# A gated weight's products cut into quarters of 256 tokens and laid between the turns of the tiles

## What is computed

```python
h = _rmsnorm(x, norm_g[layer]) * (1.0 + scale) + shift
proj = h @ w_in[layer]
(glu_a, glu_b, z_conv, q, k, v, z_att, g_conv, g_att) = jnp.split(proj, split_idx, axis=-1)
u = glu_a * jax.nn.sigmoid(glu_b)
u = lax.conv_general_dilated(u, conv_w[layer][:, None, :], window_strides=(1,), ...)
```

## Time and profile before

| what | value |
|---|---|
| median of 3 runs | 2903.88 us (2903.24 to 2905.91) |
| the profiled execution's own time | 2902.55 us |
| its span, first to last instruction | 2900.7 us |
| TensorE busy | 2809.1 us, 97% of the span |
| VectorE, ScalarE, GpSimd busy | 1783.9, 1245.5, 459.8 us |
| mean granted clock of TensorE | 0.992 of full |

### The profile page before, as it was taken

One profiled execution on the slowest core, in us unless ns is written; L12 is line 12 of the kernel. 1 busy time (PEld: TensorE's weight loads), 2 busy tenths in 40 slices (PEclk: granted clock), 3 DMA queues, 4 the chain that ended last, 5 costly groups with the idle time before them and its releaser, 6 DMA issues.

```text
span 2900.7 us, 36531 instructions
## 1 busy us (share of the span) xinstructions
PE 2809.1 (97%) x14556; PEld 2322.1 (80%) x14556; DVE 1783.9 (61%) x2498; ACT 1245.5 (43%) x2011; POOL 459.8 (16%) x423
## 2 busy tenths in 40 slices
PE   8999999999999999999988999999999999999998
PEld 7978888867884788888877888888888878588898
DVE  4645888322436788888874777777777664110564
ACT  4234787232221677777765124454443342011101
POOL 1500221000001211111114000000001063132241
PEclk9999999999999999999998999999999999999999
DMA  4130000411216999999973121030201221010141
GB/s 146 52 127 15 30 1 6 182 60 66 73 44 241 361 393 395 397 397 396 396 259 132 58 95 52 19 113 27 98 28 34 97 66 65 20 54 30 44 145 59
DMA packets 141461, 382.30 MB, mean 132 GB/s; under 512 B 11743, under 2 KB 45025, under 8 KB 141164
## 3 DMA queue, kind: packets, MB, share of 16 engines
q1 hardware_dynamic: 125036, 324.17, 29.6%
q0 software_dynamic: 13520, 46.28, 5.0%
q10 hardware_dynamic: 2736, 9.50, 0.9%
HBM read 340.47 MB, written 39.46 MB: 131 GB/s over the span
## 4 chain that ended last, share of the span: by engine, by line
PE 69%; DVE 7%; ACT 2%; issue 1%; DMA 1%; POOL 1%; ACTq 0%; POOLq 0%; DVEq 0%
PE ps L2750 7%; PE ps L2751 7%; PE ps L2752 7%; PE ps L2735 6%; PE ps L2737 6%; PE ps L2736 6%; PE ps L2365 4%; PE ps L2379 4%; PE ps L2815 2%; PE ps L2860 2%; PE ps L2817 2%; PE ps L2816 2%; PE ps L2829 1%; PE ps L2831 1%; PE ps L2830 1%
## 5 line engine op out<-in xcount | busy, mean ns | idle before, releaser
L2143 DVE SCALAR_TENSOR_TENSOR b_f<-b_f,small_f 128x1023 f32<-128x1023 f32 (+14 forms) x240 | 304.2, 1268 | 65.8 <-ACT small_f L1225 37.2
L2750 PE MATMUL ps<-x_f32r,w_f32r 128*128 128x512 f32 x480 | 187.8, 391 | 0.9 <-issue 0.8
L2752 PE MATMUL ps<-x_f32r,w_f32r 128*128 128x512 f32 x480 | 186.8, 389 | 0.0
L2736 PE MATMUL ps<-w_f32r,a_f32r 128*128 128x512 f32 x456 | 177.4, 389 | 0.0
L2365 PE MATMUL ps<-small_f 128*128 128x128 f32 (+1 forms) x984 | 135.5, 284 | 28.9 <-DMA b_f<-acc 11.6
L2751 PE MATMUL ps<-ht_f32r,w_f32r 128*128 128x512 f32 x416 | 161.9, 389 | 0.0
L2816 PE MATMUL ps<-w_f32r,a_f32r 128*128 128x512 f32 x384 | 150.0, 391 | 0.0
L2365 PEld LDWEIGHTS ps<-small_f 128*128 128x128 f32 (+1 forms) x984 | 117.5, 144 | 38.5 <-DMA b_f<-acc 12.0
L2750 PE MATMUL ps<-ht_f32r,w_f32r 128*128 128x512 f32 x320 | 124.9, 390 | 2.4 <-DVE x_f32r L2117 2.4
L2752 PE MATMUL ps<-ht_f32r,w_f32r 128*128 128x512 f32 x320 | 124.5, 389 | 0.0
L2736 PE MATMUL ps<-x_f32r,a_f32r 128*128 128x512 f32 x312 | 121.6, 390 | 0.0
(11 more groups left out here) (508 smaller groups left out, 7905.1 us busy)
## 6 DMA issues: line engine op xcount, KB each, us to landing
w_f<-in_w_exp_up SPq DMA_DIRECT2D x40, 1024.0 KB, 9.5
w_f<-in_w_exp_down SPq DMA_DIRECT2D x38, 1024.0 KB, 8.4
w_f<-in_w_exp_gate SPq DMA_DIRECT2D x36, 1024.0 KB, 8.0
x_f<-in_w_exp_gate SPq DMA_DIRECT2D x28, 1024.0 KB, 8.0
x_f<-in_w_exp_down SPq DMA_DIRECT2D x26, 1024.0 KB, 9.5
x_f<-in_w_exp_up SPq DMA_DIRECT2D x24, 1024.0 KB, 9.4
w_f<-in_w_in SPq DMA_DIRECT2D x22, 1024.0 KB, 5.1
w_f<-in_w_in SPq DMA_DIRECT2D x10, 2048.0 KB, 7.8
```

The source lines that it names most:

```text
L2143: ins = v.scalar_tensor_tensor(C_conv[k][:, d:S], U_conv[k][:, 0:S - d], cols[:, k, R_TAP + j:R_TAP + j + 1], C_conv[k][:, d:S], ALU.mult, ...
L2736: mm(o, x1, w2[:, k, c], start=False, stop=False)
L2750: mm(o, l1, r1, start=(k == 0), stop=False)
L2752: ins = mm(o, l2, r1, start=False, stop=(k == n - 1))
```

## The change

Weight 0's products are cut into quarters of 256 tokens (q = 0 to 3). Each quarter of each of its four (name, c) pairs is 24 matmuls of 128x256 into one half of a bank; the quarters 0 and 1 share the bank of h = 0, the quarters 2 and 3 that of h = 1. TensorE's new order: behind the turns of tile 2 come the two b quarters 0, behind those of tile 3 the two a quarters 0, behind tile 4 b 1, behind tile 5 a 1, behind tile 6 b 2, behind tile 7 a 2, and then all four quarters 3. A quarter q waits for `n4_split` 4(q + 1), that is for the tiles 2q and 2q + 1. Spare turns stay only ahead of the tiles 0 to 2. The turns use the banks 4 to 7 alone, so that the quarters have the banks 0 to 3 (and 4 and 5 for a of h = 1). ScalarE takes the two sigmoids of h = 0 behind its copies of tile 5. VectorE's program stays as it is.

```diff
--- before.py
+++ after.py
@@ -444,13 +444,22 @@
 
         GLU = [(nm, 0, c, h) for h in range(2) for nm in "ba" for c in range(2)]
         GLU += [(nm, i, c, h) for i in range(1, 4) for nm in "ba" for c, h in QUAD]
+        QUARTER = [(nm, c) for nm in "ba" for c in range(2)]
+
+        def quarter_steps(t):
+
+
+            q, part = divmod(t - 2, 2)
+            return [] if t < 2 else [(nm, c, q) for nm, c in QUARTER[2 * part:2 * part + 2]]
+
+        QUARTER_BANK = {("b", 0): (0, 0), ("b", 1): (1, 1), ("a", 0): (2, 4), ("a", 1): (3, 5)}
         for t in range(T):
-            if t >= T // 2:
-                nm, i, c, h = GLU[t - T // 2]
-                bk.add((f"glu_{nm}", i, c, h), bank=t - T // 2)
             for j in range(2):
-                bk.add(("n4", t, j), bank=2 * t + j if t < T // 2 else 4 + 2 * (t % 2) + j)
-        for nm, i, c, h in GLU[T // 2:]:
+                bk.add(("n4", t, j), bank=4 + 2 * (t % 2) + j)
+            for nm, c, q in quarter_steps(t):
+                if q % 2 == 0:
+                    bk.add((f"glu_{nm}", 0, c, q // 2), bank=QUARTER_BANK[nm, c][q // 2])
+        for nm, i, c, h in GLU[8:]:
             bk.add((f"glu_{nm}", i, c, h))
         def keys_of(g, tile):
 
@@ -1537,6 +1546,14 @@
                     act.wait_ge(sem("n4a_ssq"), t)
                 square(XB[:, t, :], D, st[:, 84 + t:85 + t], n4_junk[min(t, 1)]).then_inc(sem("n4a_ssq"), 1)
 
+            def gated(i, pos, c, h):
+                b = bk.wait(act, ("glu_b", i, c, h))
+                n = 4 * i + pos
+                if n >= 6:
+                    bk.read(act, ("glu_a", (n - 6) // 4, *QUAD[(n - 6) % 4]))
+                ins = nc.scalar.activation(sig[n % 6], PS[:, b, :], ACT.Sigmoid)
+                bk.done(ins, ("glu_b", i, c, h))
+
             first_square(0)
             first_square(1)
             for t in range(T + 1):
@@ -1556,6 +1573,9 @@
                             kk = 4 * j + k
                             ins = nc.scalar.activation(n4_tmp[(2 * u + j) % 4][:, c], PS[:, b, c], ACT.Identity, bias=affine[:, KC + kk:KC + kk + 1], scale=affine[:, kk:kk + 1])
                         bk.done(ins, ("n4", u, j))
+                    if u == 5:
+                        for c in range(2):
+                            gated(0, c, c, 0)
             act.wait_ge(sem("n4_split"), 2 * T)
 
             def chunk_out(k, part):
@@ -1580,12 +1600,8 @@
                     if i == 3 and pos == 2:
                         bk.read(act, ("glu_a", 2, 1, 0)), bk.read(act, ("glu_a", 2, 1, 1))
                         chunk_out(5, U[5])
-                    b = bk.wait(act, ("glu_b", i, c, h))
-                    n = 4 * i + pos
-                    if n >= 6:
-                        bk.read(act, ("glu_a", (n - 6) // 4, *QUAD[(n - 6) % 4]))
-                    ins = nc.scalar.activation(sig[n % 6], PS[:, b, :], ACT.Sigmoid)
-                    bk.done(ins, ("glu_b", i, c, h))
+                    if i > 0 or h > 0:
+                        gated(i, pos, c, h)
                 if i < 3:
                     first_hi(2 * i + 2)
                 else:
@@ -2765,23 +2781,38 @@
 
             def glu(nm, i, c, h):
                 split_wait(f"g{nm}{i}")
-                if i == 0:
-                    if c == 0 and nm == "b":
-                        spare_turns((f"glu_{nm}", i, c, h), 30)
-                    pe.wait_ge(sem("n4_split"), T + T * h)
                 feature_major((f"glu_{nm}", i, c, h), f"g{nm}{i}", c, h, ht_1)
 
+            def glu_quarter(nm, c, q):
+                h, part = divmod(q, 2)
+                name = (f"glu_{nm}", 0, c, h)
+                split_wait(f"g{nm}0")
+                pe.wait_ge(sem("n4_split"), 4 * (q + 1))
+                if part == 0:
+                    bk.begin(pe, name)
+                o = PS[:, bk.at[name][0], 256 * part:256 * part + 256]
+                w1, w2 = split_views(f"g{nm}0")
+                x1, x2 = (x[:, :, 256 * q:256 * q + 256] for x in ht_1)
+                for k in range(KC):
+                    mm(o, w1[:, k, tile(c)], x1[:, k, :], start=(k == 0), stop=False)
+                    mm(o, w1[:, k, tile(c)], x2[:, k, :], start=False, stop=False)
+                    ins = mm(o, w2[:, k, tile(c)], x1[:, k, :], start=False, stop=(k == KC - 1))
+                if part == 1:
+                    bk.end(ins, name)
+
             for t in range(T):
-                if t >= T // 2:
-                    glu(*GLU[t - T // 2])
                 if t == 0:
                     pe.wait_ge(sem("x_tile0"), XB_IN)
-                if t < T // 2:
-                    spare_turns(("n4", t, 0), 38 if t == 0 else 12)
+                if t < 3:
+                    spare_turns(("n4", t, 0), (38, 12, 12)[t])
                 pe.wait_ge(sem("n4b_hn"), t + 1)
                 for j in range(2):
                     turns(("n4", t, j), HN[t % 2][:, NB * j:NB * j + NB])
-            for g in GLU[T // 2:]:
+                for step in quarter_steps(t):
+                    glu_quarter(*step)
+            for nm, c in QUARTER:
+                glu_quarter(nm, c, 3)
+            for g in GLU[8:]:
                 glu(*g)
 
             def gate(u):
```

## The result

The changed kernel takes 2890.14 us (median of 5 runs, 2888.15 to 2892.86), against 2905.91 (2903.24 to 2908.25) for the kernel before beside it. The ratio of the runs is 0.9948, 95% interval 0.9937 to 0.9960: 15.1 us less, 11.6 to 18.3. Forecast were 2889.4 us and 14.5 less.

The account below looks back on a forecast made before the run. TensorE bounds the kernel, busy for 97% of the span. Quarters 46.1, turns 4.6 and clock 0.8 sum to 51.5 us against 66.0, so weight 1 starts 14.5 earlier: 2889.4 us, range 2885.5 to 2894.

Parts of the forecast that it names:

- The start: Norm stage: quarter 0 starts at 1543.45, just behind VectorE's last split of tile 1, which ends at 1543.42.
- The price of 256 columns: Quarters on TensorE: 384 matmuls 0.120 us apart cost 46.1, which is 2.5 more than the 43.6 of the halves.
- Rival 4: Quarters run at another rate: gain gone above 0.158 us between starts; at 1.2 GHz 46 more, 2935.4 us; chance 0.04.
- Turns: TensorE's turns of tiles 3 to 7 cost 0.92 us each, 4.6 in all.
- The clock: Quarter 0: its first 1.6 us run at half rate, losing 0.8 us; bounds 0 and 1.7 more.
- The sign "granted clock 1.00 from about 1545 on": Listed among the signs of a right forecast: TensorE at full clock from about 1545 us, early in the quarters.
- S: Stretch from tile 1's last split to weight 1's first product: 66.0 us before, predicted 51.5.
- Covers: Norm stage: splits, scaled tiles, banks and the sigmoids' table load are ready in time, so TensorE never waits for them.
- rival 1: ScalarE's chain stops TensorE now and then: 4.5 us lost, 2893.9 us; chance 0.15 together with VectorE's lateness not being absorbed.
- the thinnest slack: Weight 1's split takes 5.0 us after the last b quarter, TensorE needs it after 5.76: slack 0.75.
- What is behind the stage moves along: Behind weight 0, VectorE's sum and the v weight's fetch move along; nothing is tied to a time of its own.
- Rival 3: Something behind the stage, a fetch or the v weight, has its own time: no gain, 2903.9 us; chance 0.03.

Follow-up runs that it names:

- e2: Changed kernel with ScalarE's two sigmoids of h = 0 behind the copies of tile 6 instead of tile 5; 6.1 us less than the kernel before.
- e5: Changed kernel with the last four quarters in the order a, a, b, b instead of b, b, a, a; 6.1 us less than the kernel before.
- e6: Changed kernel with four convolution taps moved from weight 2's stretch to weight 1's, making VectorE late; median 2890.11 us.
- e1: Changed kernel with h = 1 products whole again behind tile 7's turns, after 30 spare turns; 8.4 us less than the kernel before.
- e7: Changed kernel without the stage's 38, 12 and 12 spare turns; 2890.07 us.
- e3: Changed kernel with 28 instead of 12 spare turns ahead of tile 2's turns and 6 behind them; median 2887.71 us.

## Why the prediction was right

- **The start.** Quarter 0 starts 0.10 behind the last split of tile 1 (1545.88 against 1545.78), where the prediction had 0.03.
- **The price of 256 columns.** Starts are 0.120 apart (1549.32, 1549.44), 384 of them 46.1. The term stands; that the 2.5 us over the halves is the price of loading the weights twice as often, as the prediction says, is not shown by any run. The formula of the Trainium skill that was weighed against it (TensorE: Matmul & The Clock Gate, "Back-to-back issue gap", 0.109) doesn't describe this stream; the row decides. That section of the Trainium skill gives the formula for a single matmul by itself, which the prediction leaves out. The estimate by the formula, 16.5, was 2.4 above the 14.1 of the profile. Rival 4 would have needed 0.158. Its price for the whole stage at the half clock was too high: it doubled 0.120 to 0.240, but the slow starts are 0.213 apart, and the slow turns that it leans on are 0.204 to 0.115, not twice. With 0.213 the loss would be 36 and not 46.
- **Turns.** A lap is 6.63; without its 5.76 it is 0.87, five times 4.4, against 4.6.
- **The clock.** Predicted 0.8, measured 1.4: 16 matmuls at 0.213 in the changed kernel. The size was off by 0.6: in the profile of before the half rate began with the turns of tile 2 (0.204 each), here those eight still took 1.09 in all and the half rate fell wholly on the first quarter. It is within the bounds given, as are the 0.5 to 2.4 of the other executions. The sign "granted clock 1.00 from about 1545 on" did not come: it was 0.50 from 1546 to 1548, and the slow starts end at 1549.2. That is the clock of 0.50 within the quarters that was to point to rival 4, but it lasted for 3.3 us of the 52.
- **Sum.** 46.1 + 4.4 + 1.4, with the 0.1 at the start, are 52.0, which is S; predicted 51.5.
- **Covers.** All held, and rival 1 with its waits did not come. The splits were ready in time, the table load is hidden (e2 shows by how little: one place later and 4.55 are idle), the thinnest slack is 0.84 against 0.75 (e5 shows what stands behind it). VectorE's last multiplication of weight 0 starts at 1601.17, 3.4 behind its product, and 0.44 of idle time is left at 1625.34; e6 shows that even without it nothing is lost.
- **What is behind the stage moves along.** VectorE's sum of the two parts and ScalarE's v weight, the rows of the changed kernel (VectorE, then ScalarE):

```profile
1723.23 0.69 DVE L2180 TENSOR_TENSOR b_f<-ps,a_f 128x512 f32<-128x512 f32 x1 [4.75 <-PE ps L2768]
...
1729.83 4.43 DVE L2207 TENSOR_TENSOR ht_f<-ht_f32r,x_f32r 128x4096 f32<-128x4096 f32 x1
```

```profile
1738.42 1.06 ACT L1627 ACTIVATE b_f32r<-w_f 128x1024 fp32r<-128x1024 f32 x1 [17.76 <-DMA w_f<-in_w_in]
```

The sum comes 11.7 earlier on the clock of the trace, that is 14.1 less the late start of 2.4; the v weight 11.4 earlier. Rival 3 is out. The same wait for the fetch is there (17.76 for 17.50): it hangs on a product and came along.

That the median landed 0.7 us from the forecast is partly luck: S was 0.5 longer than predicted, the clock's part of it can come out 1 us to either side in another execution, and the kernel before ran at 2905.91 in the larger set of runs, 2.0 above the median that the forecast started from.

## What to carry to other kernels

When the busiest engine waits in a stage that comes tile by tile, count its work and its waits separately: the most a new order can give is the waits, and it gives them if at every step the next piece's inputs are ready within a lap of work. Cutting products to half their width is cheap where the distance of starts nearly halves (0.227 to 0.120, 2.5 us for 384 matmuls), since it lets work start two tiles earlier. Then look for what the old wait hid: here a sigmoid with its table load and the split of the next weight, whose places had about 2 us and 0.8 us to spare. And when two profiles differ by a microsecond or two, first take out what each lost to the clock.

## What the hardware showed that I had not expected

- Nearly the same wait of TensorE (2.04 us before, 2.06 after, in the window stage) was followed by the full clock in one profile (1.00 at 1928 to 1931) and by the half clock in the other (0.64 at 1917 to 1920), at a cost of 1.6 us. Work that only moved by some us can gain or lose that much far away from the change.
- TensorE's half-clock stretch at the start of the quarters has no fixed length for one program: from the first matmul it took 3.3 us until the clock was back at full in the changed kernel, 1.2 in e2, 1.4 in e5, 5.0 in e1 and 5.5 in e6. In e7, after 20.34 us of idle time and then 24 turns at the half clock with waits between them, it took 1.4, as in e5.
- Spare turns ahead of an idle gap of 2.2 us did not hold the clock (changed kernel, e1, e2, e5 and e6); in e3's profile, where spare turns left only 0.48 and 0.43 of the idle time, it held.
